# Attention's first scores wait for four banks instead of eight, two small chains move into its first units, and the output projection's first three chunks move ahead of a normalisation

## The reference, cut to what matters

```python
h = _rmsnorm(x, norm_attn[layer])
proj = h @ w_in[layer]
# four mixers of four heads each, head width 64:
# stick-breaking, block attention with bias, a three-branch one (compressed, selected, window), differential
o_df = _rmsnorm(o_df, diff_subln[layer]) * (1.0 - lambda_init)
mixed = jnp.concatenate([o_sb, o_mb, o_ns, o_df], axis=-1)
x = x + mixed @ w_out[layer]
h2 = _rmsnorm(x, norm_mlp[layer])
x = x + jnp.square(jax.nn.relu(h2 @ w_up[layer])) @ w_down[layer]
```

## Time and profile before

| What | Value |
|---|---|
| median of 3 runs | 2364.28 us (2363.65 to 2364.48) |
| the profiled execution's own time | 2365.65 us |
| its span, first to last instruction | 2363.5 us |
| PE busy | 2255.5 us, 95% of the span |
| DVE busy | 1354.2 us, 57% |
| ACT busy | 1194.4 us, 51% |
| mean granted TensorE clock | 0.995 |
| layer 0: four transposes to the chunks of `out` | 91.3 to 183.1 us from the start |
| layer 1: the same | 469.3 to 559.7 us |

### The profile page before, as it was taken

The page is one execution under the profiler, slowest core; times in us unless marked ns, Lnnn a source line. Parts: engine busy times, 40 slices in busy tenths (PEclk is TensorE's granted clock), DMA queues, the critical chain, the costliest instruction groups (busy, mean ns, idle before and its releaser), DMA issues.

```text
span 2363.5 us, 33820 instructions
## 1 busy us (share of the span) xinstructions
PE 2255.5 (95%) x13592; PEld 1859.8 (79%) x13592; DVE 1354.2 (57%) x2252; ACT 1194.4 (51%) x2020; POOL 12.2 (1%) x10
## 2 busy tenths in 40 slices
PE   8999999999999899999999999999999997899998
PEld 7759999957999777787676666867777876658998
DVE  5665655666665665445556555356565346446774
ACT  4556545555554563444344342256565335546764
POOL 0000000000000000000000000000000000000000
PEclk9999999999999999999999999999999999999999
DMA  7864544793445213222121121222222222204542
GB/s 296 324 251 143 183 174 179 281 361 125 175 165 185 85 69 107 89 89 90 53 89 54 72 72 47 96 72 89 90 89 98 99 89 73 106 19 156 184 163 106
DMA packets 45721, 312.31 MB, mean 132 GB/s; under 512 B 4951, under 2 KB 7255, under 8 KB 8580
## 3 DMA queue, kind: packets, MB, share of 16 engines
q1 hardware_dynamic: 45572, 310.20, 36.3%
HBM read 309.11 MB, written 1.07 MB: 131 GB/s over the span
## 4 chain that ended last, share of the span: by engine, by line
PE 80%; DVE 10%; ACT 7%; issue 2%; DMA 1%; ACTq 0%; SPq 0%; DVEq 0%
PE bank L757 56%; PE bank L762 8%; DVE ws L1694 3%; ACT ws L1236 2%; PE bank L966 2%; PE bank L1127 2%; DVE xs L1719 2%; PE bank L1027 1%; PE bank L1098 1%; PE bank L830 1%; PE bank L952 1%; PE bank L951 1%; PE bank L1008 1%; DVE arena L2104 1%; ACT xs L1260 1%
## 5 line engine op out<-in xcount | busy, mean ns | idle before, releaser
L757 PE MATMUL bank<-xs,ws 128*128 128x256 f32 (+1 forms) x9648 | 1570.0, 324 | 60.7 <-DVE xs L1719 48.9
L757 PEld LDWEIGHTS bank<-xs,ws 128*128 128x128 f32 x9648 | 1398.4, 191 | 234.0 <-DVE xs L1719 65.5
L1694 DVE TENSOR_TENSOR ws<-ring,ws 128x1024 fp32r<-128x1024 f32 x464 | 550.9, 1228 | 278.6 <-ACT ws L1236 278.4
L1236 ACT ACTIVATE ws<-ring 128x1024 fp32r<-128x1024 f32 x464 | 464.6, 1049 | 287.0 <-PE bank L757 279.2
L1719 DVE TENSOR_TENSOR xs<-arena,xs 128x512 fp32r<-128x512 f32 (+1 forms) x286 | 166.8, 599 | 305.6 <-ACT xs L1260 304.7
L1260 ACT ACTIVATE xs<-arena 128x512 fp32r<-128x512 f32 (+1 forms) x286 | 148.9, 538 | 338.1 <-PE bank L757 224.6
L762 PE MATMUL bank<-ws,xs 128*128 128x512 f32 (+1 forms) x1008 | 230.2, 388 | 6.3 <-ACT arena L1495 2.2
L1719 DVE TENSOR_TENSOR xs<-hT,xs 128x512 fp32r<-128x512 f32 (+1 forms) x216 | 133.0, 619 | 178.5 <-ACT xs L1260 178.5
L762 PEld LDWEIGHTS bank<-ws,xs 128*128 128x128 f32 x1008 | 188.5, 189 | 46.8 <-DVE xs L1719 3.2
L1260 ACT ACTIVATE xs<-hT 128x512 fp32r<-128x512 f32 (+1 forms) x216 | 122.8, 575 | 199.0 <-PE bank L757 190.3
L1716 DVE SCALAR_TENSOR_TENSOR xs<-xT,par,xs 128x256 fp32r<-128x256 f32 x112 | 51.1, 479 | 14.5 <-ACT xs L1258 11.9
(11 more groups left out here) (263 smaller groups left out, 1479.0 us busy)
## 6 DMA issues: line engine op xcount, KB each, us to landing
ring<-in_stream SPq DMA_DIRECT2D x233, 1024.0 KB, 4.8
arena<-in_side SPq DMA_DIRECT2D x56, 1024.0 KB, 7.0
arena<-bias_vectors SPq DMA_DIRECT2D x1, 1536.0 KB, 10.4
hT<-in_tokens SPq DMA_DIRECT2D x1, 1024.0 KB, 6.3
arena<-in_tokens SPq DMA_DIRECT2D x1, 1024.0 KB, 13.5
out<-arena SPq DMA_DIRECT2D x2, 512.0 KB, 3.1
arena<-in_params SPq DMA_DIRECT2D x1, 918.0 KB, 9.7
arena<-bias_vectors SPq DMA_DIRECT2D x1, 706.0 KB, 11.8
```

The lines of the kernel that those rows point to most:

```text
L757: ins = mm(ps(n, c, c + g.T), a[wi][:, p * P:(p + 1) * P], x[xi], start=first, stop=last)
L1236: do(ws[:, i % 2, 0, c], ring[:, w % R, c], ACT.Copy).then_inc(w_high, 1)
L1694: ins = v.tensor_tensor(ws[:, i % 2, 1, c], ring[:, w % R, c], ws[:, i % 2, 0, c].bitcast(F32), ALU.subtract)
```

## The change

It applies to both layers.

1. Ahead of the loop PE waits for the four banks of the second half of `proj` alone; the four of `nat` are waited for in turn 3, ahead of the first product with values.
2. DVE's small chains move into the loop: copy and gelu argument behind the scores of unit 0, the scalar and the gates behind the scores of unit 1, the gelu's end from turn 1 to turn 2. ACT's exp of the gelu moves behind unit 0.
3. Chunk 0 of `out` goes into PE's turn 29, chunk 1 into turn 30, and chunk 2 between the loop and `dfn`. Chunks 3 to 7 follow `dfn`. The four tickets of `out` move to turn 29.
4. ACT feeds chunks 0 and 1 at the end of turn 28 (`i == NU`), DVE right behind its loop. Chunk 2 is fed where it was. DVE now waits for one bank (the last output's) there instead of eight.

```diff
+            if i == NU + 1:
+                n.add(("out", l), 4)
...
-        n.add(("out", l), 4)
...
-                for n in range(N(("hidT", l)) - BANKS + 1, N(("hidT", l)) + 1):
+                for n in range(N(("proj", l, 1)), N(("proj", l, 1)) + 4):
                     pe.wait_ge(bank_free[n % BANKS], n // BANKS + 1)
...
+                    if i > NU:
+                        linear(G("out", l), i - NU - 1, i - NU)
+                    if i == 3:
+                        for n in range(N(("nat", l)), N(("nat", l)) + 4):
+                            pe.wait_ge(bank_free[n % BANKS], n // BANKS + 1)
...
+                linear(G("out", l), 2, 3)
                 n = N(("dfn", l))
                 pe.wait_ge(sq_ready, seen(sq_ready))
...
-                linear(G("out", l))
+                linear(G("out", l), 3)
...
-                act_.wait_ge(gelu_arg, l + 1)
-                do(hid, hidg, ACT.Exp, scale=-2.0 * math.sqrt(2.0 / math.pi)).then_inc(gelu_exp, 1)
                 for i in range(NU + 3):
+                    if i == 1:
+                        act_.wait_ge(gelu_arg, l + 1)
+                        do(hid, hidg, ACT.Exp, scale=-2.0 * math.sqrt(2.0 / math.pi)).then_inc(gelu_exp, 1)
...
+                    if i == NU:
+                        feed_to(G("out", l).q0 + 1)
...
-                    if i == 1:
+                    if i == 2:
                         dve.wait_ge(gelu_exp, l + 1)
...
+                feed_to(G("out", l).q0 + 1)
...
-                for n in range(N(("O", l, NU - 1)) - BANKS + 1, N(("O", l, NU - 1)) + 1):
-                    dve.wait_ge(bank_free[n % BANKS], n // BANKS + 1)
+                n = N(("O", l, NU - 1))
+                dve.wait_ge(bank_free[n % BANKS], n // BANKS + 1)
                 feed_to(G("out", l).q0 + 2)
```

More of the change, by code:

```diff
@@ L1809, in _ @@
                 ins.then_inc(bank_free[n % BANKS], 1)
-                n = N(("hidT", l))
-                dve.wait_ge(bank_full[n % BANKS], n // BANKS + 1)
-                v.tensor_copy(hid.rearrange("p a b -> p (a b)"), ps(n, 0, 64)).then_inc(bank_free[n % BANKS], 1)
-                dve.wait_ge(bank_free[n % BANKS], n // BANKS + 1)
[L1815 to L1834, removed]
                 dve.wait_ge(cbias_ready, 1)
                 for i in range(NU + 1):
-                    if i == 1:
+                    if i == 2:
                         dve.wait_ge(gelu_exp, l + 1)
@@ L1872, in _ @@
                                             ).then_inc(logits_ready, 1)
+                    if i == 0:
+                        n = N(("hidT", l))
+                        dve.wait_ge(bank_full[n % BANKS], n // BANKS + 1)
+                        v.tensor_copy(hid.rearrange("p a b -> p (a b)"), ps(n, 0, 64)).then_inc(bank_free[n % BANKS], 1)
+                        dve.wait_ge(bank_free[n % BANKS], n // BANKS + 1)
+                        gx = lamp.rearrange("p (a b) -> p a b", a=4)
+                        v.tensor_tensor(gx, hid, hid[:, :, 15:16].to_broadcast([P, 4, 16]), ALU.add).then_inc(dve_own, 1)
+                        dve.wait_ge(dve_own, own(dve_own))
+                        v.tensor_tensor(hidg, gx, gx, ALU.mult).then_inc(dve_own, 1)
+                        dve.wait_ge(dve_own, own(dve_own))
+                        v.tensor_scalar(hidg, hidg, 0.044715, 1.0, ALU.mult, ALU.add).then_inc(dve_own, 1)
+                        dve.wait_ge(dve_own, own(dve_own))
+                        v.tensor_tensor(hidg, hidg, gx, ALU.mult).then_inc(gelu_arg, 1)
+                    if i == 1:
+                        dve.wait_ge(lam_exp, seen(lam_exp))
+                        v.tensor_tensor(lam[:, 4:5], lam[:, 3:4], lam[:, 2:3], ALU.subtract)
+                        v.tensor_scalar(lam[:, 6:7], par_at(("subln", l)), 1.0 - lam_init, None, ALU.mult).then_inc(dve_own, 1)
+                        dve.wait_ge(dve_own, own(dve_own))
+                        v.tensor_scalar(lam[:, 5:6], lam[:, 4:5], -lam_init, None, ALU.add)
+                        dve.wait_ge(gate_exp, seen(gate_exp))
+                        v.tensor_scalar(lam[:, 16:40], lam[:, 16:40], 1.0, None, ALU.add).then_inc(dve_own, 1)
+                        dve.wait_ge(dve_own, own(dve_own))
+                        v.reciprocal(lam[:, 16:40], lam[:, 16:40]).then_inc(dve_own, 1)
+                        dve.wait_ge(dve_own, own(dve_own))
+                        gates = lam[:, 16:40].rearrange("p (a b) -> p a b", a=2)
                     if i >= 1:
```

2 lines of the change are left out of this document (1 added, 1 removed).

## The result

| What | Before | Changed |
|---|---|---|
| median (lowest to highest of 5 runs each) | 2364.28 us (2360.13 to 2368.02) | 2377.04 us (2374.83 to 2380.95) |
| ratio, 95% interval | | 1.0058 (1.0045 to 1.0071) |
| profiled execution, own time | 2365.65 us | 2377.04 us |
| its span | 2363.5 us | 2375.0 us |
| PE busy | 2255.5 us | 2260.2 us |

The changed kernel is slower by 0.58%, 2377.0 us where 2376.1 was forecast. In what follows its lines have moved by up to ten: L952 is the first scores (L951 before), L1009 the transposes (L1008), L1033 and L1034 the products with values, L1043 `dfn` (L1036), L758 the chunks, L868 the sums behind `out` (L867), L1267 and L1729 the two halves of an input's split.

The account below looks back on a forecast made before the run. The prediction took PE to bound the kernel. Per layer -1.0 (start) + 5.8 (end) + 1.1 (clock) = +5.9, both layers +11.8 us, gave 2376.1 us against the median 2364.28; range 2371.5 to 2380.5.

Parts of the forecast that it names:

- The start: Start of attention's loop: PE's 1.08 us wait ahead of the first scores goes; -1.0 us per layer.
- (a): End of the loop: PE waits 1.0 us ahead of chunk 0, fed by ACT behind an output's copy.
- (b): PE waits 2.05 us ahead of chunk 2, whose feed stands behind the last output's copy and the squares.
- (c): PE waits 3.24 us between `dfn` and chunk 3, which ACT and DVE feed only after `dfn_ready`.
- the sign it gave: Three PE waits per layer at the end, about 1.0, 2.0 and 3.2 us, all ended by DVE's split.
- (d): PE waits 0.4 us ahead of chunk 4, which needs the next weight slot.
- The end without the clock: Sum at the loop's end: (a), (b), `dfn`'s 1.12, (c) and (d), less the old 2.05; +5.8 us per layer.
- (e): One fall of the granted clock to 0.50 per layer, behind the wait of (c); +1.1 us per layer.
- more falls: Rival: the wait of (b) may bring a clock fall too, over chunk 2; 2379.1 us, chance 0.14.
- No fall of the clock: Rival: the waits are there, but the clock does not fall; 2373.9 us, chance 0.22.
- The end even: Rival: waits (a) to (c) are no more than what they replace; 2362.3 us, chance 0.08.
- Faster: Rival: chunks fill PE's wait before `dfn`, and chunk 3 is ready when `dfn` ends; 2359.9 us, chance 0.03.

Follow-up runs that it names:

- x0early: As `both`, but chunk 0 alone is fed in turn 20, chunks 1 and 2 behind turn 28; 2358.05 us, ratio 0.9987.
- warm: Changed kernel plus dummy matmuls on constants, 4 ahead of chunk 2 and 6 behind `dfn`; 2372.98 us, ratio 1.0050.
- both: Changed kernel with the earlier feeds of `feed2` and `feed34` together; 2360.32 us, ratio 0.9988.
- feed2: Changed kernel with chunk 2 fed along with chunks 0 and 1, ahead of the last output's copy; 2370.21 us, ratio 1.0029.
- feed34: Changed kernel with chunk 3 fed ahead of the normalisation's Ln and Exp, chunk 4 ahead of the wait for its end; 2366.84 us, ratio 1.0015.
- end_only: Changed kernel with parts 1 and 2 taken back, so the start is as before; 2377.11 us, ratio 1.0061.
- turn20: As `both`, but chunks 0 to 2 and their weight slot are fed in turn 20; 2373.50 us, ratio 1.0032.

## Why the prediction was right, and where not

**The start** (-1.0 per layer): measured -1.12. The first scores follow the transposes, and the reordered chains of DVE had more room than the sum gave them: 0.44 us between the end of ACT's exp and PE's transposes, where the working had 0.25 (0.15 behind a hop of 0.1). No load was late.

**(a)** 1.0 us, measured 0.80. **(b)** 2.05, measured 2.08. **(c)** a wait of 3.24, measured 3.21 and 3.20. These three were ended by what the prediction named, but the sign it gave, a wait ended by DVE's split, holds for (b) and (c) alone; (a) is shown by `x0early`. **(d)**, 0.4 us, was mis-sized: no run has a wait of PE ahead of chunk 4, and with the clock whole it cost 0.04 us (`warm`). PE's waits grew by 0.80 + 2.08 + 3.21 - 1.13 = 4.96 us. The end without the clock was put at +5.8 us and came out at +6.05, near it although 0.4 of the 5.8 was (d). What the sum lacked is that a wait costs more than the idle time in its bracket, which begins at the modelled end of the instruction before; without a wait the next one starts ahead of that end. From the start of one thing to the start of the next, chunk 0 comes 1.35 us after the transposes and 0.30 in `x0early` (177.86 - 176.51, 177.85 - 177.55); chunk 2 comes 2.47 us after the last product and 0.31 in `both` (185.65 - 185.34); chunk 3 comes 4.22 us after `dfn` in `warm` (194.95 - 190.73) and 0.46 in `both` (189.08 - 188.62). That is 1.05 + 2.16 + 3.76 = 6.97 us above the 34.96 of `x0early`, which has no wait: 41.93, and `warm` measured 41.95. The method that gave these is worth a word: each wait was the length of an old path, read from the rows of the kernel before, put behind a new starting point. `feed2` and `feed34` confirm which path it was.

**(e), the clock, is the other term that was mis-sized.** It had one fall of 3.41 us per layer behind (c), 1.5 us, less the hidden 0.4. In the changed kernel's profile the falls at (c) are twice as long, 6.82 us, and cost 2.3 us each beyond the waits; layer 0 has one over chunk 2 too, which was the rival of more falls. Together 6.1 us at the two ends, where the prediction had 2 x 1.1 = 2.2 net. In the profile of `end_only` the falls at (c) have the forecast length, 3.41 us, and cost 1.2 us each (24.84 against 23.67), and with the one over chunk 2 it is 3.7 us. So the size differs from execution to execution, and at (c) `end_only` has about what was forecast. The sum still came within a microsecond because two other things went the other way, neither foreseen: the falls behind the waits of 2.10 us were missing in this execution (-2.9 us), and the program's start was 1.5 us shorter. 2 x (6.05 - 1.12) + 6.1 - 2.9 - 1.5 = 11.6, against a span that grew by 11.5 us. Without those two, the change's own parts in this trace come to 15.9 us, where 11.8 was forecast. So the waits were right for the reasons given, and the nearness of the total is partly luck.

**The rivals.** No fall of the clock: refuted by the stretches above; that the falls come of the waits is supported by `warm`. It is also what the Trainium skill, "TensorE: Matmul & The Clock Gate", section on HAM oscillation, would have here, for it warns of longer idle gaps only. The prediction's "by that page" goes by this section alone, and waits of 3.2 us lie close under the gap that it names. The shorter ones disagree with it clearly: 0.50 was granted behind waits of 2.08, 2.10 and, in `turn20`, 1.73 us. More falls: half true, in one layer of two. The end even: refuted, 45.76 against 35.90 us. Faster: refuted for this change, yet its condition was the right one. It said that a feed of chunk 3 ahead of `dfn_ready` was needed, and with that and chunk 2's feed `both` loses the two long waits.

**What stays open.** Why a wait of one length is followed by a fall in one place or execution and not in another. The waits behind the attention of each layer and the length at a granted clock of 0.50 at each, one profiled execution per kernel:

| Kernel | ahead of chunk 2, layers 0 and 1 | behind `dfn`, layers 0 and 1 |
|---|---|---|
| changed | 2.08 us: 3.41, none | 3.2 us: 6.82, 6.82 |
| `end_only` | 2.09 and 2.08 us: 3.41, none | 3.20 us: 3.41, 3.41 |
| `feed34` | 2.09 and 2.08 us: none, 3.41 | no wait |
| `feed2` | no wait | 3.31 us: 3.41, none |
| `warm` | filled: none, none | filled: none, none |

So three of six waits of 2.1 us and five of six of 3.2 or 3.3 us met a fall, and none of four that were filled. Three rows of these: the stretch of `end_only` in layer 0 and that of `feed34` in layer 1, and PE's timeline of `feed2` in layer 1, where the 192 matmuls take 23.66 us behind the longest of the waits:

```profile
198.89:202.30 3.41, 3.41 (x19) 3.41 (x18) 2.00 (x4) 0.86 (x3) 0.00 (x0) 0.50 0.29 43
565.77:569.18 3.41, 3.41 (x17) 3.41 (x18) 2.46 (x3) 1.41 (x2) 0.00 (x0) 0.50 0.00 0
573.46 23.66 PE L758 MATMUL bank<-xs,ws 128*128 128x256 f32 x192 [3.31 <-DVE xs L1729]
```

The waits of 2.10 us of the kernel before behave alike: a fall then, none in the changed kernel's profile, though both waits are still there.

That such falls go with the spread of the times, the record does show: of the 35 runs of the kernel before in group 2, the fastest, 2358.16 us, has a mean clock of 0.998, and the six from 2367.09 us up all have 0.994. That the long slow stretches of `turn20` last because the matmuls there are small was not tried by itself.

## What to carry to other kernels

When work is moved ahead of a long chain of small steps, ask what covered the chain before: the three chunks moved here were the cover of `dfn`'s path, and moving them to fill 1.13 us opened 3.2. An order of work on the bound engine is only as good as the order in which the other engines feed it; both waits went by feeding chunks 2 to 4 earlier, where ACT and DVE had been idle for some 6 us. And a wait of the matrix engine is to be priced above its own length: 0.80 us cost 1.06 here, and from 2.1 us on a slow clock came on top at eight of twelve waits.

## What the runs showed of the hardware

- A granted clock of 0.50 came with waits of PE of 1.73, 2.08, 2.10 and 3.2 us, but not with each (8 of the 12 waits tabled above). In chunks of 256-column matmuls it lasted 3.41 us (1.2 to 1.5 us lost) or 6.82 us (2.3 us lost beyond the wait).
- With matmuls on constants in such waits the clock stayed at 1.00 at all four; between the marks that was 3.8 and 2.3 us less than in the changed kernel's profile, but the times of whole runs don't separate the two.
- In `turn20`, in a stretch of small matmuls behind a wait of 1.73 us, the clock stayed at 0.50 for 20.5 and 23.9 us while PE was busy throughout. From the four transposes to `dfn` layer 0 took 9.9 us longer than in `both`, wait included. By the mean clocks this came in eight of 12 runs, in six of them as strongly as in the profile.
- A wait of PE delayed the next chunk by more than its idle time: 0.80 us by 1.05, 2.08 us by 2.16, 3.31 us by 3.87 (`feed2` against `both`).
